# Three branch output projections as three fp32r products each, their weights split piece by piece beside the gates

## The reference, cut to what matters

```
h = modulate(rmsnorm(x), sh1, sc1)
u = h @ w_in                                  # 2048 -> 3584 branch columns + 4 * 2048 gate columns
y_a = pool_mixer(...)                         # 4 groups of 128 channels, each @ (128 x 512)
y_b = conformer_conv(...) @ conf_w_out        # (256 x 512) @ (512 x 2048)
y_c = short_conv(...)     @ sc_w_out          # (256 x 512) @ (512 x 2048)
y_d = fourier_mixer(...)  @ fnet_w_out        # (256 x 512) @ (512 x 2048)
merged = sum_k sigmoid(gate_k) * y_k
x = x + gt1 * (merged @ w_o)
```

## Time and profile before

| what | value |
|---|---|
| median of 3 runs | 1859.7 us (1859.21 to 1860.25) |
| profiled execution, own time | 1858.33 us |
| its span | 1856.5 us |
| mean granted TensorE clock | 0.981 |
| PE busy | 1763.9 us (95%) |
| DVE busy | 899.4 us (48%) |
| ACT busy | 393.7 us (21%) |
| HBM read | 639.20 MB |

### The profile page before, as it was taken

How to read it: one execution, slowest core, us unless ns; L and a number is a source line. 1 busy time by engine, 2 the same in 40 slices (tenths; PEclk the granted TensorE clock), 3 DMA queues, 4 the chain that set the end, 5 groups by cost and what they waited for, 6 DMA issues and landing times.

```text
span 1856.5 us, 26120 instructions
## 1 busy us (share of the span) xinstructions
PE 1763.9 (95%) x10306; PEld 1016.1 (55%) x10306; DVE 899.4 (48%) x1087; ACT 393.7 (21%) x477; POOL 0.9 (0%) x5
## 2 busy tenths in 40 slices
PE   1979999999999999999999999999999999999996
PEld 1868747786777677687444444444444443434342
DVE  5876766866757644457432333333233332323334
ACT  3010014432322333334211101111011111101011
POOL 0000000000000000000000000000000000000000
PEclk8989999989989999999999999999999999999998
DMA  9996597779868945355699999999999999999995
GB/s 374 386 387 257 191 378 291 295 274 351 303 249 317 339 151 212 148 189 237 247 422 422 422 422 422 422 422 422 423 421 422 422 422 422 422 423 421 422 422 237
DMA packets 137004, 641.92 MB, mean 346 GB/s; under 512 B 8578, under 2 KB 8706, under 8 KB 76674
## 3 DMA queue, kind: packets, MB, share of 16 engines
q1 hardware_dynamic: 136256, 637.08, 86.2%
q10 hardware_dynamic: 562, 2.55, 0.4%
q0 software_dynamic: 144, 1.70, 0.2%
HBM read 639.20 MB, written 2.10 MB: 345 GB/s over the span
## 4 chain that ended last, share of the span: by engine, by line
PE 68%; DMA 24%; DVE 6%; ACT 1%; issue 1%; SPq 0%; DVEq 0%; ACTq 0%
DMA ring<-in_exp_w 19%; PE ps L925 16%; PE ps L889 6%; PE ps L658 5%; PE ps L659 5%; PE ps L660 5%; PE ps L628 5%; DVE r_m L1296 4%; PE ps L912 3%; PE ps L867 3%; PE ps L571 3%; PE ps L584 3%; DMA ring<-in_branch_w 2%; DMA ring<-in_ada_w 2%; PE ps L753 2%; PE ps L754 2%
## 5 line engine op out<-in xcount | busy, mean ns | idle before, releaser
L925 PE MATMUL ps<-ring 128*64 128x512 f32 x2048 | 464.8, 596 | 5.8 <-DMA ring<-in_exp_w 5.8
L925 PEld LDWEIGHTS ps<-ring 128*64 128x64 f32 x2048 | 143.1, 137 | 291.7 <-issue 291.7
L1664 DVE TENSOR_TENSOR r_h<-r_h,ps 128x1024 f32<-128x1024 f32 x124 | 145.8, 1218 | 205.8 <-PE ps L912 205.8
L659 PE MATMUL ps<-g_lo,h_hi 128*128 128x512 f32 x512 | 201.7, 394 | 0.0
L1637 DVE TENSOR_TENSOR r_c<-ps,scale 128x512 f32<-128x512 f32 x65 | 44.7, 688 | 292.6 <-PE ps L867 291.7
L1209 ACT ACTIVATE r_m<-ps 128x512 f32<-128x512 f32 x32 | 19.1, 597 | 697.7 <-PE ps L925 697.7
L658 PE MATMUL ps<-mix_hi,h_hi 128*128 128x512 f32 x384 | 157.9, 411 | 0.0
L1095 ACT ACTIVATE mix_hi<-ring 128x1024 fp32r<-128x1024 f32 x96 | 101.7, 1062 | 261.1 <-PE ps L660 261.1
L1403 DVE TENSOR_TENSOR g_lo<-ring,mix_hi 128x1024 fp32r<-128x1024 f32 x96 | 117.5, 1225 | 77.7 <-ACT mix_hi L1095 76.9
L660 PE MATMUL ps<-mix_hi,h_lo 128*128 128x512 f32 x384 | 151.6, 395 | 0.0
L867 PEld LDWEIGHTS ps<-r_c,xparts 128*128 128x128 bf16 x3120 | 108.8, 118 | 50.9 <-issue 49.5
(11 more groups left out here) (267 smaller groups left out, 1745.8 us busy)
## 6 DMA issues: line engine op xcount, KB each, us to landing
ring<-in_exp_w SPq DMA_DIRECT2D x320, 1024.0 KB, 20.2
ring<-in_w_in SPq DMA_DIRECT2D x40, 2048.0 KB, 10.1
r_b<-in_exp_w SPq DMA_DIRECT2D x64, 1024.0 KB, 22.1
ring<-in_ada_w SPq DMA_DIRECT2D x24, 2048.0 KB, 18.7
ring<-in_ada_w SPq DMA_DIRECT2D x48, 1024.0 KB, 5.1
ring<-in_w_o SPq DMA_DIRECT2D x8, 2048.0 KB, 7.7
ring<-in_w_in SPq DMA_DIRECT2D x12, 1024.0 KB, 14.9
ring<-in_branch_w SPq DMA_DIRECT2D x6, 2048.0 KB, 9.7
```

Of the source, the lines that this page charges most:

```text
L659: mm(ps[:, b + t, :], h, lo[:, cols], start=False, stop=False)
L925: last = mm(ps[m * NWIN:(m + 1) * NWIN, 2, :], xe[:, k, :], chunk(2 * c + m)[:, kk * F:(kk + 1) * F], start=(k == 0), stop=(k == KT - 1))
L1664: V.tensor_tensor(x1n, x1n, ps[:, (6, 4)[b]:(6, 4)[b] + 2, :].rearrange("p b n -> p (b n)"), ALU.add).then_inc(added, 1)
```

## The change

The outputs y of g = 1, 2 and 3 are no longer made in fp32 but in three fp32r products, as the gates are. The activations of a branch (128 x 1024) are split once for each branch: ACT writes the high part in iteration i = 2 of unit j = 0, DVE the low part in i = 3, in place. The high part of g goes into an area whose branch is no longer used. The weights are split for each unit in four pieces of 128 x 512: pieces k = 0, 1, 2 in i = 5, 6, 7 behind the gate piece, with three buffers for high parts, and piece 3 after the loop. Piece 3 takes the buffer of piece 0 and so waits for PE's products with piece 0 (`bw_used`); on ACT it stands behind the sigmoid. The low part of a piece is left in place in slot BW. The wait for the branch's load moves from PE to ACT, ahead of piece 0's split. PE's loop over k is now the outer one, and before each k it waits for the low part of that piece. ACT's loop over g = 1, 2 is written out instead of a loop on the engine. Two small tables of the router are stored apart, to make room for the third high buffer.

```diff
+        br_r = at("br_r", [P, N_BRANCH, MT, S], F32R, (N_SLOT + 1) * SLOT * 4)
+        bw_lo = at("bw_lo", [P, 4, 2 * MIX], F32R, BW * SLOT * 4)
+        bw_pair = at("bw_pair", [P, 2, MIX], F32R, 147456 + 7168 * 4)
+        bw_third = sb("bw_third", [P, MIX], F32R)
+        bw_hi = [bw_pair[:, 0, :], bw_pair[:, 1, :], bw_third[:, :]]
...
-                    if j % 2 == 0:
-                        pe.wait_ge(bw_in, 16 * (2 * (g - 1) + j // 2 + 2))
...
+                        pe.wait_ge(br_parts, g)
-                    last = gate_y(n, MT, lambda k, t: brT[:, g, k, t * P:(t + 1) * P],
-                                  lambda k: bw[:, k, (j % 2) * MIX:(j % 2 + 1) * MIX])
-                    last.then_inc(y_done, 1)
+                    for k in range(MT):
+                        pe.wait_ge(bw_lo_done, 16 * (g - 1) + 4 * j + k + 1)
+                        hi, lo = bw_hi[k % 3], bw_lo[:, k, (j % 2) * MIX:(j % 2 + 1) * MIX]
+                        for t in range(TT):
+                            toks = slice(t * P, (t + 1) * P)
+                            mm(ps[:, y_bank(n) + t, :], br_high(g)[:, k, toks], hi, start=(k == 0), stop=False)
+                            mm(ps[:, y_bank(n) + t, :], br_high(g)[:, k, toks], lo, start=False, stop=False)
+                            last = mm(ps[:, y_bank(n) + t, :], br_r[:, g, k, toks], hi, start=False, stop=(k == MT - 1))
+                        last.then_inc(bw_used if k < 3 else y_done, 1)
...
+            def branch_high(g):
+                act.wait_ge(y_done, 4 * g)
+                act.wait_ge(conf_ready, MT)
+                A(br_high(g), brT[:, g, :, :], ACT.Copy).then_inc(br_hi_done, 1)
+            def branch_w_high(g, j, k):
+                if k == 0 and j % 2 == 0:
+                    act.wait_ge(bw_in, 16 * (2 * (g - 1) + j // 2 + 2))
+                if k == 3:
+                    act.wait_ge(bw_used, 12 * (g - 1) + 3 * j + 1)
+                else:
+                    act.wait_ge(y_done, 4 * g + j)
+                A(bw_hi[k % 3], slot(BW)[:, k * 1024 + (j % 2) * MIX:k * 1024 + (j % 2 + 1) * MIX], ACT.Copy
+                  ).then_inc(bw_hi_done, 1)
...
+                        i = x - 8 * j - AHEAD
+                        if g and j == 0 and i == 2:
+                            branch_high(g)
+                        if g and i >= 5:
+                            branch_w_high(g, j, i - 5)
...
                     A(tmp[n % 2], ps[:, u_bank(n):u_bank(n) + 2, :], ACT.Sigmoid).then_inc(unit_saved, 1)
+                    if g:
+                        branch_w_high(g, j, 3)
...
+            def branch_w_low(g, j, k):
+                v.wait_ge(bw_hi_done, 16 * (g - 1) + 4 * j + k + 1)
+                V.tensor_tensor(bw_lo[:, k, (j % 2) * MIX:(j % 2 + 1) * MIX],
+                                slot(BW)[:, k * 1024 + (j % 2) * MIX:k * 1024 + (j % 2 + 1) * MIX],
+                                bw_hi[k % 3].bitcast(F32), ALU.subtract).then_inc(bw_lo_done, 1)
...
                         if not last and i % 2 == 1:
                             ada_one(g, 4 * j + i // 2)
+                        if j == 0 and i == 3:
+                            v.wait_ge(br_hi_done, g)
+                            V.tensor_tensor(br_r[:, g, :, :], brT[:, g, :, :], br_high(g).bitcast(F32), ALU.subtract
+                                            ).then_inc(br_parts, 1)
+                        if i >= 5:
+                            branch_w_low(g, j, i - 5)
+                    branch_w_low(g, j, 3)
```

More of the change, by code:

```diff
@@ L150, in build, with br_high @@
         m_lo = at("m_lo", [P, KT, S], F32R, 147456)
+        br_r = at("br_r", [P, N_BRANCH, MT, S], F32R, (N_SLOT + 1) * SLOT * 4)
[3 more added lines that the diff above has]
+        bw_hi = [bw_pair[:, 0, :], bw_pair[:, 1, :], bw_third[:, :]]
+        def br_high(g):
+            return br_r[:, (g - 1) % 2, :, :]
         g_hi = [mix_hi[:, 0, :], mix_hi[:, 1, :], mix_hi[:, 2, :], pad_hi[:, :]]
@@ L185, in build @@
         rs = sb("rs", [P, 16, TT])
-        ct = sb("ct", [32, 2, P])
+        ct = sb("ct", [32, P])
+        n_win = sb("n_win", [32, 1])
         stp = sb("stp", [P, NE])
@@ L214, in build @@
         g_used = sem("g_used")
+        br_hi_done = sem("br_hi_done")
+        br_parts = sem("br_parts")
+        bw_hi_done = sem("bw_hi_done")
+        bw_lo_done = sem("bw_lo_done")
+        bw_used = sem("bw_used")
         m_hi_done = sem("m_hi_done")
@@ L664, in _ @@
             pw = slot(BW)[:, 0:2048].rearrange("p (q n) -> p q n", q=4)
-            bw = slot(BW).rearrange("p (k n) -> p k n", k=4)
             for j in range(4):
@@ L843, in _ @@
             pe.wait_ge(cnt_ready, 1)
-            mm(ps[:, 0, 128:160], ct[:, 0, :], tri[0:32, 0:32], start=True, stop=True).then_inc(start_done, 1)
+            mm(ps[:, 0, 128:160], ct[:, :], tri[0:32, 0:32], start=True, stop=True).then_inc(start_done, 1)
             first_rest(1, 1, 3)
@@ L945, in _ @@
             pe.wait_ge(cnt_ready, 2)
-            mm(ps[0:32, 1, 224:225], tri[0:32, 0:32], ct[:, 0, 0:1], start=True, stop=True)
-            mm(ps[0:32, 1, 225:226], tri[0:32, 0:32], ct[:, 1, 0:1], start=True, stop=True).then_inc(start_done, 1)
+            mm(ps[0:32, 1, 224:225], tri[0:32, 0:32], ct[:, 0:1], start=True, stop=True)
+            mm(ps[0:32, 1, 225:226], tri[0:32, 0:32], n_win[:, :], start=True, stop=True).then_inc(start_done, 1)
             pe.wait_ge(lo_ready, 8)
@@ L956, in _ @@
                    stop=(w == MAXWIN - 1))
-            mm(ps[0:1, 1, 384:385], ones[0:32, 0:1], ct[:, 1, 0:1], start=True, stop=True)
+            mm(ps[0:1, 1, 384:385], ones[0:32, 0:1], n_win[:, :], start=True, stop=True)
             for w in range(MAXWIN):
@@ L1079, in gate @@
                             wo_high(x - 32)
+                        i = x - 8 * j - AHEAD
[3 more added lines that the diff above has]
+                            branch_w_high(g, j, i - 5)
                     n = N_UNIT + j
                     act.wait_ge(g_used, 8 * (j + 1) + 32 * g)
-                    if not (isinstance(g, int) and 4 * g + j < 2):
+                    if 4 * g + j >= 2:
                         act.wait_ge(y_saved, 4 * g + j - 1)
                     A(tmp[n % 2], ps[:, u_bank(n):u_bank(n) + 2, :], ACT.Sigmoid).then_inc(unit_saved, 1)
+                    if g:
+                        branch_w_high(g, j, 3)
                     if last and j > 0:
@@ L1114, in _ @@
                 gate_high(0, x)
-            gate(0, False)
-            with act.Fori(1, N_BRANCH - 1) as g:
+            for g in range(N_BRANCH - 1):
                 gate(g, False)
@@ L1580, in _ @@
             v.wait_ge(pos_done, 1)
-            V.tensor_copy(ct[:, 0, :], ps[0:32, 0, 0:P]).then_inc(cnt_ready, 1)
+            V.tensor_copy(ct[:, :], ps[0:32, 0, 0:P]).then_inc(cnt_ready, 1)
             v.wait_ge(cnt_ready, 1)
@@ L1584, in _ @@
             active, first_w, off_w, cnt_w = (ec[:, i * MAXWIN:(i + 1) * MAXWIN] for i in range(4))
-            count = ct[:, 0, 0:1].broadcast_to([32, MAXWIN])
+            count = ct[:, 0:1].broadcast_to([32, MAXWIN])
             step(V.tensor_tensor(active, count, c_over, ALU.is_gt))
-            V.tensor_reduce(ct[:, 1, 0:1], active, AX_X, ALU.add).then_inc(cnt_ready, 1)
+            V.tensor_reduce(n_win[:, :], active, AX_X, ALU.add).then_inc(cnt_ready, 1)
             v.wait_ge(start_done, 1)
```

## The result

The changed kernel takes 1866.19 us (median of 6 runs, 1863.64 to 1868.25), the kernel before 1859.01 on the same chip (6 runs, 1857.37 to 1860.25). The ratio is 1.0038, with an interval of 1.0027 to 1.0049: slower by 0.4%. Predicted were 1864.7 us. The profiled execution of after took 1864.40 us, 1862.6 of it span, 6.1 us more than the one of before.

What follows compares the result with a forecast made beforehand. Before the load-bound experts' stage, a chain mostly over PE was taken as the bound, carried one for one to the end. Late units +13.8, early -3.1, g = 3 -5.7 gave +5.0 us: 1864.7 us median, range 1856 to 1876.

Steps and rivals of the forecast that it cites:

- Late units: Four units where y waits for branch_w's landing: `ada_one` stands before the third piece, 3.46 us lost each, +13.8 us.
- Early units: Units j = 1 and 3 of g = 1, 2, load long there: 0.78 us saved each, not 1.42; -3.1 us.
- g = 3: Four units without `ada_one`, loads in time: y saves the full 1.42 us each, -5.7 us.
- The splits' sizes: One 512-wide split of branch weights: 0.58 us on ACT, 0.61 to 0.69 on DVE; cost hardly matters in late units.
- The clock in the late units: TensorE's clock in PE's gaps around y: no fall taken, 0 us; 0 to 11 us kept as possible loss.
- the 2.5 that I named as a sign: In late units PE would idle some 2.5 us before the third piece, with DVE named as releaser.
- The sums: Partition sums after g = 1 and g = 2: 7.40 and 3.63 us; a clock fall costs 3.8, gate 2 to 3.
- Rival (c): Clock kept in the sum after g = 1: 5.0 - 6.6 = -1.6 us, 1858.1, no change; chance 0.19.
- Rival (b): Late units' splits follow the landing at PE's pace, only the first shows: -11.6 us, 1848.1; chance 0.09.
- R + 6.3: Late units: faster if the third piece is split before this; R is y's start on PE in the kernel before.

Runs made afterwards that it cites:

- e1: Changed kernel with the fourth `ada_one` of a unit (i = 7) moved behind the four splits; 1855.3 us, ratio 0.9978 to the kernel before.
- e2: Changed kernel with the branch's load issued earlier, between the two pairs of ada_w tiles of its unit; 1843.67 us, ratio 0.9917 to the kernel before.
- e6: As e1, with the first three pieces split together in i = 5, ahead of gate splits i = 6 and 7; 1854.05 us, ratio 0.9969 to the kernel before.
- e4: Changed kernel with three-product y in g = 3 alone, g = 1 and 2 in fp32; 1857.67 us, ratio 0.9988 to the kernel before.
- e9: Changed kernel with the partition sums' 128 operand columns taken side by side, not one in four; 1857.34 us in a single run.
- e5: Changed kernel with the edits of e1 and e2 together; 1837.8 us, ratio 0.9885 to the kernel before.
- e8: e5 with the partition sums of g = 0, 1, 2 spread among the next unit's gate products; 1828.78 us, ratio 0.9838 to the kernel before.

## Why the prediction was right, and which of its steps were not

- **Late units** (+13.8 expected, +13.4 measured). The step held in its order and to 0.1 us: the third piece at R + 7.60 (433.55 - 425.94 = 7.61), y's end at R + 10.43 (10.49, and 10.48 or 10.49 in the three other units too). The Trainium skill (TensorE: Matmul & The Clock Gate, Architectural detail) has ACT and DVE as strict queues; the trace agrees, `bw_lo` of the third piece starts only behind `ada_one`. e1 shows the cause, since it moves this one instruction and gains 11 us, and e2 shows that the cause needs the late landing. The units differ only by the landing. SP issues 8.42 us before E in all four units of both kernels, as the prediction had it; from the issue to R it is 9.56, 9.57, 10.76 and 9.81 us in after, and 11.05, 9.84, 9.71 and 9.75 in before. So (1,0) is +2.03 and (2,0) +4.56, and the sum is 4 x 3.52 - 0.65 = 13.4; the 0.65 us, in which the landings came sooner in this profile, were in no term of the prediction.
- **Early units** (-3.1, -2.7). A gap of 0.44 us was there. I had y 6.08 us long; it is 6.20.
- **g = 3** (-5.7, -5.4). 24 products at 0.2285 make 5.48 us, not 5.44. So three terms save 20% of the fp32 form's 6.87 us: one fp32r product takes 0.2285 us, and a quarter of an fp32 one (6.87 / 32) 0.215. The Trainium skill (FP8 and Floating Point Precision, TensorE Precision Notes) has a true fp32 product as four passes; the estimate from that, a saving of 25%, is met by no y here.
- **The splits' sizes** (0.58 on ACT, 0.69 on DVE) measured 0.61 to 0.63 and 0.68 to 0.69. They made no difference.
- **The clock in the late units** is the step that failed. I took "no fall", from the 2.47 us in the earlier trace rows; it fell in all four (0.50 in 430 to 432, 562 to 564 and 624 to 626, 0.56 in 492 to 494). It cost nothing, for the reason that I had given for a fall before the first piece: the slow products are those of pieces 0 and 1, and PE would have waited for DVE anyhow. PE's wait before the third piece is therefore 1.2 to 1.5 us, not the 2.5 that I named as a sign. In e1 and e6, where DVE is quicker, the same fall costs: y ends 0.6 to 0.9 us later in e1's units with a fall than in the one without, and 1.4 to 1.5 later in e6's. My value rested on the gap of 2.47 us in one unit, and e4 against before shows that it is no rule.
- **The sums.** I read the 7.40 and 3.63 us of the earlier trace rows as one block at two clocks. That is wrong: e9, and the stretches beside it, show that the first two blocks are long because of the operand's stride, at either clock. What the clock costs is 1.5 to 3 us in the gate behind a block, and 0.7 in a block whose columns lie side by side (4.22 us in e5, where it fell inside the third block). After the third sum the clock held in before and fell in after:

```profile
664.00:666.00 2.00, 2.00 (x7) 1.61 (x6) 2.00 (x2) 0.00 (x0) 0.00 (x0) 0.60 1.02 420
666.00:668.00 2.00, 2.00 (x6) 1.53 (x5) 0.99 (x1) 0.34 (x1) 0.00 (x0) 0.54 0.35 143
```

  That is +1.56 us in unit (3,0); the two others came out 0.4 better each. Rival (c) had 6.6 us to win here; the 3.8 of the block were not to be had, since a strided block is as long at full clock.
- **The rest of the difference.** The profiled run lies 6.1 us over that of before, and the units give 5.3. The medians differ by 7.2, and profiles of one kernel scatter by the falls of the clock, 1.5 to 3 us each; more than that the comparison can't tell.

Rival (b), the change as it was meant, did not come in. The prediction says that the change is faster from where the third piece is split before R + 6.3. e1 has it at R + 5.2 and is faster, after at R + 7.6 and is slower: both fit, though they don't fix the point.

## What to carry to other kernels

When a wait for a transfer is moved from the engine that uses the data to an engine that prepares it, everything queued behind it there comes late too. Write down what stands between the landing and the last prepared piece, and move long work that nobody waits for (here an accumulation of 2.35 us) behind it. Better still, first issue the load earlier: in this kernel the two made of +7 us one of -22, and the issue alone was worth more than the order. A wait of 1 us on a PE that is the bound deserves that look before the products are made cheaper.

## What I had not expected of the hardware

- A stationary operand of 128 x 128 fp32 that is read as one column in four loads in 329 ns, at a clock of 1.00 and of 0.50 alike (the stretches of after, beside e9). Side by side it loads in 192 ns at 1.00, and in 333 ns at 0.50, as at the end of e5's third block:

```profile
L704 PEld LDWEIGHTS ps<-keep,r_m x7: 308/333/333, 632.9 to 634.1; 128*128 128x128 f32 x7
```

  A block of 16 products of one column (32 instructions) so takes 7.5 us against 3.5 to 3.6 at full clock, and the lower clock lengthens only the second kind.
- The clock fell in or behind a block of one-column products while PE was busy 2.00 of every 2 us: for all three blocks of after and of e5, for two of the three in before and in e9. Spread between gate products, the same work left it at 1.00 in all three places (e8).
- Gaps of the same length at the same place were followed by a fall in one kernel and not in another: 2.40 us fell in e4 and not in before, 1.95 in e4 against 1.93 in before. Of the gaps between 1.9 and 3 us in the profiles some were followed by a fall (2.55 in after, 2.67 in e1) and some were not (2.66 in e1, 2.88 and 2.93 in e6). What decides is open.
